# DMA transposes of the f16 parts of the probabilities in a two-layer hybrid attention encoder

## The chip, the cores and the metric

The kernel runs on one core of a Trainium2 chip, in one launch. The metric is the device time in microseconds; of the kernel before there are three runs, with a median of 2575.91 us (2571.5 to 2578.02).

## What is computed

An encoder of two layers runs for two requests: 512 tokens ("prompt") and 1024 tokens ("sample"), both of width 1024. All inputs are f32. Per layer:

```python
mod = jax.nn.silu(c) @ w_ada + b_ada
shift, scale, gate = jnp.split(mod, 3, axis=-1)
h = rms_norm(x, g_norm) * (1 + scale[:, None, :]) + shift[:, None, :]
proj = h @ w_in      # q_lat, kv_lat, k_rope, z_a, q_b, k_b, v_b, z_b
...
oa = block_attention(qa[:, :, None], ka, va, MLA_SCALE)      # 8 heads, keys of 96, values of 64
ya = heads_to_tokens(oa) * jax.nn.silu(z_a)
...
ob = block_attention(qb, kb, vb, GQA_SCALE)      # 8 heads of 64 over 2 key heads
yb = heads_to_tokens(ob) * jax.nn.silu(z_b)
out = jnp.concatenate([ya, yb], axis=-1) @ w_out
return x + gate[:, None, :] * out
```

`block_attention` is a full softmax over all keys, `softmax(q k^T * scale) v`, without a mask. A final RMSNorm follows the second layer.

## The kernel before

**Passes and tiles.** The work is four passes, `inst`: 0 is layer 0 of the prompt (512 keys), 1 is layer 0 of the sample (1024 keys), 2 and 3 are layer 1 of the same. A pass first makes keys and values for all its tokens (`key_steps`) and then goes through its query tiles of 128 tokens: 4 in a short pass, 8 in a long one (`over_tiles`, first tile, a loop of inner ones, last tile). Each engine has a program of its own, written by hand, in which the same loops run; semaphores tie them together. Nothing schedules the instructions but their order in those programs and the tables ahead of them.

**A head in a tile.** A tile has 16 slots, one per head: heads 0 to 7 are the latent attention (scores in f32, "A"), 8 to 15 the grouped-query attention (scores in f16 parts, "B"). In slot h of a long pass PE turns the probabilities of head h (`turn`, transposes of 128x128 f32 blocks through `ident` into two PSUM banks from `T_BANK`, four to a bank), forms the scores of head h+2 (`scores`), and multiplies the turned probabilities with V (`mix`, L770: three matmuls for each 128 keys, of high x high, high x low and low x high f16 parts). VectorE takes the row maximum of the scores (L1002), ACT the exponential into `probs` (L1163). ACT then copies the turned block as f16 into the high half of `PT` (`move_pt`, L1171) and VectorE writes the difference as f16 into the low half (`move_pt`, L1019). In a short pass `mix` runs one slot behind.

**Side products.** Between these stand the tile's other products, by tables of slots: z_a and z_b (gates of this tile), `out0`, `out1` (output projection of the tile before, in halves), and `PREPARE`, the queries of the next tile: h^T0 and h^T1 (transposes of the normed rows `xn`), q_lat, q_b, q_lat^T, q_up0 and q_up1, q_a^T and q_b^T. An entry stands before or after "|", that is ahead of or behind `mix` in its slot. All of them use the one PSUM bank `SIDE`; `side` makes PE wait on `mm_free` until VectorE has emptied it (`query_out`: L882 for h^T, L968 for the gates after ACT's tanh L1147, L973 for q_up). In VectorE's program the early entries of a slot stand ahead of the row maximum and the late ones behind it.

**Queues.** SP issues every DMA: a tile's rows into `xn` (L499, behind h^T1), its residual rows into `x_out` (L504), the result rows out (L507), and in the last tile of a pass the next pass's key weights (`key_weights`, with `query_weights` at the change of the layer). POOL norms and rotates the queries and forms the gates.

The line numbers in the rows: L577 is `product` (scores and side products), L567 the transpose helper (`turn`, h^T, q_a^T, y^T), L571 transposes of f16, L770 `mix`, L1028 the gated outputs, L1035 the final rows.

## Time and profile before

| | us |
|---|---|
| median of three runs | 2575.91 |
| span of the profiled execution | 2575.7 |
| PE busy | 2396.8 |
| VectorE busy | 1343.9 |
| ACT busy | 974.0 |
| POOL busy | 789.5 |
| one inner tile, 1024 keys (pass 1 / pass 3) | 92.40 / 93.45 |
| one inner tile, 512 keys (pass 2) | 72.24 |

The profiled execution's span is all that the page gives of its time; it lies 0.2 us under the median of the runs, and outside it nothing is counted. A tile here runs from one slot's product to the same one in the next tile, read from the chain. The page gives the busy time of each engine and the chain of work that ended last; windows of one tile, the chain's single pieces and a timeline around one place show what stands behind the shares.

### The profile page before, as it was taken

Reading aid. Unit: us, or ns where it says so; the run is one execution under the profiler, and the core shown is the slowest. Engines: PE = TensorE matmul, PEld = TensorE weight load, DVE = VectorE, ACT = ScalarE, POOL = GpSimd, SP = SyncE. Lnnn points to the kernel's source line nnn. Section 1 sums busy time; section 2 is a strip of 40 time slices with the busy share of each in tenths; the row PEclk is TensorE's granted clock in tenths of the full one; section 3 lists DMA queues with packets and bytes.
Section 4 is the critical chain, followed back from the end, with each engine's and each line's share of the span. In section 5 each row is a group of like instructions: output and inputs, shape, how many; then the busy total and the mean of one; then the engine's idle time right before and its main releaser. Section 6 shows DMA issues by size and latency. Waiting matters only on the chain.

```text
span 2575.7 us, 44323 instructions
## 1 busy us (share of the span) xinstructions
PE 2396.8 (93%) x16106; PEld 1409.9 (55%) x16106; DVE 1343.9 (52%) x2390; ACT 974.0 (38%) x2202; POOL 789.5 (31%) x1325
## 2 busy tenths in 40 slices
PE   6689999899999999999989899979899999999997
PEld 1344554455566566666555455545556656656654
DVE  0444444375656565555545444537555556555563
ACT  0223333133444444444422333422344444444442
POOL 0454321274421231232116632237442123123210
PEclk9799999899999999999999999999999999999999
DMA  7621112121000000000242000023000000000001
GB/s 237 222 96 58 54 52 85 58 94 38 9 9 25 16 24 8 24 17 0 73 155 98 9 17 25 33 101 122 9 9 10 33 24 16 24 33 25 0 25 41
DMA packets 63228, 129.42 MB, mean 50 GB/s; under 512 B 6687, under 2 KB 31365, under 8 KB 63125
## 3 DMA queue, kind: packets, MB, share of 16 engines
q1 hardware_dynamic: 63128, 128.09, 14.3%
q8 instruction: 64, 1.05, 0.2%
q14 instruction: 36, 0.29, 0.0%
HBM read 115.44 MB, written 12.63 MB: 50 GB/s over the span
## 4 chain that ended last, share of the span: by engine, by line
PE 75%; DVE 15%; issue 5%; ACT 2%; POOL 1%; DMA 1%; DVEq 0%; SPq 0%; POOLq 0%; ACTq 0%
PE psum L577 58%; PE psum L567 10%; PE psum L770 6%; DVE region L1019 3%; DVE nmax L1002 3%; DVE hT L882 3%; ACT region L1171 1%; DVE region L977 1%; DVE region L1028 0%; DVE region L979 0%; POOL region L1225 0%; PE psum L571 0%; ACT region L1147 0%; DVE KTa L944 0%; DMA Wq<-in_w_ada 0%
## 5 line engine op out<-in xcount | busy, mean ns | idle before, releaser
L1171 ACT ACTIVATE region<-psum 128x512 f16<-128x512 f32 x640 | 353.5, 594 | 769.2 <-PE psum L567 769.2
L577 PE MATMUL psum<-Wq,hT 128*128 128x512 f32 (+1 forms) x1536 | 611.0, 544 | 1.6 <-DVE hT L882 0.6
L1019 DVE TENSOR_TENSOR region<-psum,region 128x512 f16<-128x512 f32 x640 | 415.6, 682 | 293.4 <-ACT region L1171 292.8
L567 PE MATMUL psum<-ident,region 128*128 128x128 f32 (+1 forms) x3208 | 436.9, 277 | 21.5 <-DVE Va L917 10.5
L1002 DVE TENSOR_REDUCE nmax<-psum 128x1 f32<-128x1024 f32 (+1 forms) x384 | 398.6, 1038 | 41.9 <-PE psum L577 41.1
L577 PEld LDWEIGHTS psum<-Wq,hT 128*128 128x128 f32 x1536 | 285.0, 191 | 245.5 <-issue 224.9
L567 PEld LDWEIGHTS psum<-ident,region 128*128 128x128 f32 (+1 forms) x3208 | 356.5, 140 | 105.7 <-issue 78.6
L577 PE MATMUL psum<-Wout,region 128*128 128x512 f32 x768 | 354.5, 607 | 8.5 <-DVE region L987 6.7
L577 PE MATMUL psum<-KTa,region 96*128 96x512 f32 x640 | 311.9, 603 | 18.6 <-DVE region L977 12.9
L1225 POOL TENSOR_TENSOR region<-region,rope_sb 128x64 f32<-128x64 f32 (+3 forms) x384 | 158.3, 434 | 337.7 <-DVE region L973 321.3
L1163 ACT ACTIVATE region<-psum,nmax,unscale 128x1024 f32<-128x1024 f32 (+1 forms) x192 | 204.4, 1064 | 141.7 <-DVE nmax L1005 141.3
L1225 POOL TENSOR_TENSOR rsum<-sums,v_scale 128x8 f32<-128x8 f32 x48 | 9.7, 203 | 775.0 <-ACT region L1163 775.0
L577 PEld LDWEIGHTS psum<-Wout,region 128*128 128x128 f32 x768 | 143.9, 194 | 163.4 <-issue 145.4
L1163 ACT ACTIVATE region<-psum,nmax 128x1024 f32<-128x1024 f32 (+1 forms) x192 | 186.9, 973 | 114.1 <-DVE nmax L1002 112.2
L770 PEld LDWEIGHTS psum<-Vb,region 128*128 128x128 f16 x3840 | 136.6, 98 | 120.1 <-DVE region L1019 50.1
L770 PEld LDWEIGHTS psum<-Va,region 128*128 128x128 f16 x3840 | 136.7, 98 | 112.7 <-DVE region L1019 53.9
L770 PE MATMUL psum<-Vb,region 128*128 128x64 f16 x3840 | 152.6, 194 | 26.2 <-DVE region L1019 13.4
L577 PE MATMUL psum<-KTb,region 128*128 128x512 f16 x640 | 169.5, 379 | 1.2 <-DVE region L961 1.2
L577 PE MATMUL psum<-region,hT 128*128 128x416 f32 x384 | 149.5, 545 | 20.5 <-DVE hT L882 20.3
L968 DVE SCALAR_TENSOR_TENSOR region<-region,psum 128x512 f32<-128x512 f32 x48 | 33.0, 688 | 251.7 <-ACT region L1147 251.7
L577 PEld LDWEIGHTS psum<-KTa,region 96*128 96x128 f32 x640 | 108.7, 192 | 93.5 <-issue 81.0
L770 PE MATMUL psum<-Va,region 128*128 128x64 f16 x3840 | 148.3, 193 | 10.6 <-DVE region L1019 5.9
(110 smaller groups left out, 2156.3 us busy)
## 6 DMA issues: line engine op xcount, KB each, us to landing
Wout<-in_w_out SPq DMA_DIRECT2D x8, 2048.0 KB, 11.9
Va<-in_w_ada SPq DMA_DIRECT2D x12, 1024.0 KB, 5.4
Wq<-in_w_in SPq DMA_DIRECT2D x6, 2048.0 KB, 14.3
xn<-x_after_layer SPq DMA_DIRECT2D x24, 512.0 KB, 3.3
Wq<-in_w_ada SPq DMA_DIRECT2D x5, 2048.0 KB, 13.4
xn<-in_x_sample SPq DMA_DIRECT2D x16, 512.0 KB, 3.3
x_after_layer<-region SPq DMA_DIRECT2D x12, 512.0 KB, 2.6
region<-x_after_layer SPq DMA_DIRECT2D x12, 512.0 KB, 3.3
```

Of the source, the lines that this page charges most:

```text
L567: return nc.tensor.transpose(out, in_, ident[0:n, 0:n])
L577: last = nc.tensor.matmul(out, lhsTs[k], rhss[k], start=k == 0, stop=k == n - 1)
L770: last = nc.tensor.matmul(out, PT[:, a, pt_block(h, S, c), :], v, start=c == 0 and a + b == 0, stop=c == NT - 1 and a == 1)
L882: last = nc.vector.tensor_scalar(hT[:, k, :], ps[:, j * P:(j + 1) * P], gs[:, m, k:k + 1], cols[:, 16 * m + k:16 * m + k + 1], ALU.mult, A ...
L968: last = nc.vector.scalar_tensor_tensor(out=half, in0=half, scalar=1.0, in1=ps, op0=ALU.add, op1=ALU.mult)
L977: last = nc.vector.tensor_copy(QTa[0:QK, 4 * c:4 * c + 4, :], blocks[0:QK])
L1002: last = nc.vector.reduce_max(nmax[:, h:h + 1], scores_buf(h, S), AX_X, negate=True)
L1019: nc.vector.tensor_tensor(PT[:, 1, pt_block(h, S, 4 * c):pt_block(h, S, 4 * c) + 4, :], psum[:, T_BANK + b, :].rearrange("p (c n) -> p c n ...
L1163: nc.scalar.activation(probs_buf(h, S), scores_buf(h, S), ACT.Exp, bias=nmax[:, h:h + 1], scale=scale, accum_out=sums[:, h:h + 1]).then_in ...
L1171: nc.scalar.activation(PT[:, 0, pt_block(h, S, 4 * c):pt_block(h, S, 4 * c) + 4, :], psum[:, T_BANK + b, :].rearrange("p (c n) -> p c n", ...
L1225: mul = lambda out, a, b: nc.gpsimd.tensor_tensor(out, a, b, ALU.mult)
```

## The change

**The path of the probabilities.** PE no longer turns them. ACT copies the f32 exponentials from `probs` as f16 into the first half of a buffer `P16` (`high_part`), VectorE writes the f16 difference into the second half (`low_part`), and SP issues one DMA transpose of [128, 2S] f16 from `P16` into `PT` (L550), one a head: 256 of 512 KB and 128 of 256 KB in all. Room is for 2S = 2048 columns: two heads of 1024 keys, four of 512 (`buffers`). SP waits for the low part and for `pv_done` of the head that used the buffer before; each buffer has a semaphore `pt_loaded`, for which `mix` waits once, and ACT's copy of a later head waits on it too before it overwrites `P16`.

**The lead.** In slot h PE forms the scores of head h+4 (`AHEAD_SCORES`), VectorE takes the maximum of h+4 and the low part of h+2 (`AHEAD_TURN`), ACT the exponential and copy of h+3 (`AHEAD_PROBS`). `mix` runs in its own slot in all passes.

**The side products.** `PREPARE` moves one slot earlier (q_b^T stays), `LEFT_OVER` and `ADA` too; on POOL the norm of the latent and the rotations stand one slot earlier. VectorE has the outputs and the early entries ahead of the low part, then the maximum, then the late entries.

**The queues.** The loads of layer 1's modulation weights in pass 0 and the next pass's key weights (at the change of the layer the query weights with them) are issued by ACT: the latter in slot 5 of the last tile of passes 0 and 1, behind waits for the scores and for z_b. SP's loop over tiles is written out. The second half of `Wout` is loaded one key step earlier.

```diff
@@ -58,13 +58,16 @@
 FINISH = {2: "y_b^T |", 10: "| out0/0", 11: "out0/1 |", 12: "| out1/0", 13: "out1/1 |"}
 GATE_A = {0: "| z_a/0", 1: "z_a/1 |"}
 GATE_B = {2: "| z_b/0", 3: "z_b/1 |"}
-PREPARE = {4: "h^T0 |", 5: "h^T1 |", 6: "q_lat |", 7: "| q_b/0", 8: "q_b/1 |", 9: "q_lat^T | q_up0",
-           10: "q_up1 |", 12: "q_a^T0 |", 14: "q_a^T1 |", 15: "q_b^T0 | q_b^T1"}
+PREPARE = {3: "| h^T0", 4: "h^T1 |", 5: "q_lat |", 6: "| q_b/0", 7: "q_b/1 |", 8: "q_lat^T | q_up0",
+           9: "q_up1 |", 11: "q_a^T0 |", 13: "q_a^T1 |", 15: "q_b^T0 | q_b^T1"}
 TURN = {14: "| y_a^T"}
 
-LEFT_OVER = {5: "| q_b^T0@0 q_b^T1@0"}
-
-ADA = {0: "ada0 |", 7: "ada1 |", 11: "| ada2"}
+LEFT_OVER = {3: "| q_b^T0@0 q_b^T1@0"}
+
+AHEAD_SCORES, AHEAD_PROBS, AHEAD_TURN = 4, 3, 2
+P_ROOM = 2 * SMAX
...
@@ -138,8 +141,9 @@
...
-    trounds = [t // 4 for t in tiles]
-    tr_before = [sum(16 * tiles[p] * trounds[p] for p in range(q)) for q in range(len(inst))]
+    buffers = [P_ROOM // SEQS[r] for _, r in inst]
+    loads_before = [[sum(2 * HEADS * tiles[p] // buffers[p] for p in range(q) if b < buffers[p])
+                     for b in range(max(buffers))] for q in range(len(inst))]
...
@@ -280,30 +286,51 @@
...
+        def parts_buf(q, h):
+
+            S = SEQS[inst[q][1]]
+            b = h % buffers[q]
+            return P16[:, 2 * b * S:2 * (b + 1) * S]
+
+        def pt_buf(q, h):
+
+            S = SEQS[inst[q][1]]
+            b = h % buffers[q]
+            return PT[:, 2 * b * S:2 * (b + 1) * S].rearrange("p (c n) -> p c n", n=P)
+
+        def pt_value(q, i, h):
+
+            n = buffers[q]
+            return 16 * (loads_before[q][h % n] + i * (2 * HEADS // n) + h // n + 1)
+
+        def wait_pt(eng, q, i, h):
+
+            value = pt_value(q, i, h)
+            if not isinstance(value, int) or value > 0:
+                eng.wait_ge(pt_loaded[h % buffers[q]], value)
...
@@ -360,13 +387,34 @@
...
+        def load_key_weights(eng, q):
+
+            l, r = inst[q]
+            w_in_l = w_in[l].rearrange("(k p) n -> p k n", p=P)
+            eng.dma_start(Wkv[:, :, 0:KV_KB], w_in_l[:, :, C_KV:C_ZA]).then_inc(s["wkv_loaded"], 16)
+            eng.dma_start(Wkv[:, :, KV_KB:KVC], w_in_l[:, :, C_KB:C_ZB]).then_inc(s["wkv_loaded"], 16)
+            if l and r == 0:
+                query_weights(eng, l)
...
@@ -518,21 +543,26 @@
...
+                def turn(h, i):
+
+                    sp.wait_ge(s["p_low"], heads(b0, i, h))
+                    wait(sp, "pv_done", heads(b0, i, h - buffers[q]))
+                    sp.dma_start_transpose(pt_buf(q, h), parts_buf(q, h)).then_inc(pt_loaded[h % buffers[q]], 16)
+
                 def tile(i, first, last):
                     for h, names in enumerate(completed(first, last, q == 0)):
+                        if h + AHEAD_TURN < 2 * HEADS or not last:
+                            turn(h + AHEAD_TURN, i)
                         if last and h == 4 and q + 1 < len(inst):
                             first_rows(q + 1)
-                            if l < DEPTH - 1:
-                                key_weights(q + 1)
                         for name in names:
                             side(name, owner(name, i))
 
 
-                tile(0, True, False)
-                with tile_loop(sp, 1, NT - 2, rounds=(rounds, PER_SIDE + (len(ADA) if q == 0 else 0))) as i:
-                    tile(i, False, False)
-                tile(NT - 2, False, False)
-                tile(NT - 1, False, True)
+                for h in range(AHEAD_TURN):
+                    turn(h, 0)
+                for i in range(NT):
+                    tile(i, i == 0, i == NT - 1)
...
@@ -730,7 +759,7 @@
...
-                    if h in (0, 1, 4, 8):
+                    if h in (0, 4, 8):
                         pe.wait_ge(s["mm_free"], rounds.now() - later)
                     j = h - HEADS
...
@@ -761,43 +778,37 @@
...
+                    wait_pt(pe, q, i, h)
                     for c in range(NT):
-                        if c % 4 == 0:
-                            pe.wait_ge(s["pt_low"], tr_before[q] + nr * heads(0, i, h - 1) + c // 4 + 1)
-
                         for a, b in ((0, 0), (0, 1), (1, 0)):
                             v = Va[:, c, b, head, :] if head < HEADS else Vb[:, c, b, g * GD:(g + 1) * GD]
-                            last = nc.tensor.matmul(out, PT[:, a, pt_block(h, S, c), :], v, start=c == 0 and a + b == 0,
+                            last = nc.tensor.matmul(out, pt_buf(q, h)[:, a * NT + c, :], v, start=c == 0 and a + b == 0,
                                                     stop=c == NT - 1 and a == 1)
                     last.then_inc(s["pv_done"], 1)
 
                 def tile(i, first, last):
                     for h, (before_mix, after_mix) in enumerate(slots(first, last, q == 0)):
-                        turn(h, i)
-
-                        side_first = delay or any("^T" in name or "_up" in name for name in before_mix)
+
+                        side_first = any("^T" in name or "_up" in name for name in before_mix)
                         if side_first:
                             for name in before_mix:
                                 side(name, i)
-                        later = 0 if first else 1
-                        if h + 2 < 2 * HEADS:
-                            scores(h + 2, i, later)
+                        n = h + AHEAD_SCORES
+                        if n < 2 * HEADS:
+                            scores(n, i, 0 if first and n == 4 else 1)
                         elif not last:
-                            scores(h + 2 - 2 * HEADS, i + 1, later)
+                            scores(n - 2 * HEADS, i + 1, 0)
                         if not side_first:
                             for name in before_mix:
                                 side(name, i)
...
@@ -1006,19 +1016,18 @@
...
 
                 def next_max(h, i, last):
-                    if h + 2 < 2 * HEADS:
-                        row_max(h + 2, i)
+                    n = h + AHEAD_SCORES
+                    if n < 2 * HEADS:
+                        row_max(n, i)
                     elif not last:
-                        row_max(h + 2 - 2 * HEADS, i + 1)
-
-                def move_pt(h, i):
-
-                    for c in range(nr):
-                        b = c if nr == 2 else h % 2
-                        dve.wait_ge(s["pt_high"], tr_before[q] + nr * heads(0, i, h - 1) + c + 1)
-                        nc.vector.tensor_tensor(PT[:, 1, pt_block(h, S, 4 * c):pt_block(h, S, 4 * c) + 4, :],
-                                                psum[:, T_BANK + b, :].rearrange("p (c n) -> p c n", c=4),
-                                                PT[:, 0, pt_block(h, S, 4 * c):pt_block(h, S, 4 * c) + 4, :], ALU.subtract).then_inc(s["pt_low"], 1)
+                        row_max(n - 2 * HEADS, i + 1)
+
+                def low_part(h, i):
+
+                    dve.wait_ge(s["p_high"], heads(b0, i, h))
+                    parts = parts_buf(q, h)
+                    nc.vector.tensor_tensor(parts[:, S:2 * S], probs_buf(q, h), parts[:, 0:S], ALU.subtract) \
+                        .then_inc(s["p_low"], 1)
...
@@ -1039,28 +1048,26 @@
...
-                        if not delay:
-                            move_pt(h, i)
-                            for name in names[:early]:
-                                side(name, owner(name, i))
-                            next_max(h, i, last)
+                        for name in names[:early]:
+                            side(name, owner(name, i))
+                        if h + AHEAD_TURN < 2 * HEADS or not last:
+                            low_part(h + AHEAD_TURN, i)
+                        next_max(h, i, last)
                         for name in names[early:]:
...
@@ -1156,33 +1170,38 @@
...
-                    wait(act, "tr_ready", tr_before[q] + nr * heads(0, i, h - 1 - delay))
+                    wait(act, "p_low", heads(b0, i, h - buffers[q]))
                     if h % HEADS == 0:
                         wait(act, "gate_ready", 2 * (b0 + i) - 1 + h // HEADS)
                     scale = 1.0 if h < HEADS else unscale[:, l:l + 1]
-                    nc.scalar.activation(probs_buf(h, S), scores_buf(h, S), ACT.Exp, bias=nmax[:, h:h + 1], scale=scale,
+                    nc.scalar.activation(probs_buf(q, h), scores_buf(h, S), ACT.Exp, bias=nmax[:, h:h + 1], scale=scale,
                                          accum_out=sums[:, h:h + 1]).then_inc(s["exp_done"], 1)
 
-                def move_pt(h, i):
-
-                    for c in range(nr):
-                        b = c if nr == 2 else h % 2
-                        act.wait_ge(s["tr_ready"], tr_before[q] + nr * heads(0, i, h - 1) + c + 1)
-                        nc.scalar.activation(PT[:, 0, pt_block(h, S, 4 * c):pt_block(h, S, 4 * c) + 4, :],
-                                             psum[:, T_BANK + b, :].rearrange("p (c n) -> p c n", c=4),
-                                             ACT.Copy).then_inc(s["pt_high"], 1)
+                def high_part(h, i):
+
+                    wait_pt(act, q, i, h - buffers[q])
+                    act.wait_ge(s["exp_done"], heads(b0, i, h))
+                    nc.scalar.activation(parts_buf(q, h)[:, 0:S], probs_buf(q, h), ACT.Copy).then_inc(s["p_high"], 1)
+
+                def probabilities(h, i):
+                    exponentials(h, i)
+                    high_part(h, i)
+
+                def next_probabilities(h, i, last):
+                    n = h + AHEAD_PROBS
+                    if n < 2 * HEADS:
+                        probabilities(n, i)
+                    elif not last:
+                        probabilities(n - 2 * HEADS, i + 1)
...
...
-                        if not delay:
-                            move_pt(h, i)
-                        if h + 1 < 2 * HEADS:
-                            exponentials(h + 1, i)
-                        elif not last:
-                            exponentials(0, i + 1)
-                        if delay:
-                            move_pt(h, i)
+                        next_probabilities(h, i, last)
+                        if last and h == 5 and q + 1 < len(inst) and l < DEPTH - 1:
+                            act.wait_ge(s["scores_ready"], 16 * before[q + 1] - 8)
+                            act.wait_ge(s["mm_ready"], at["z_b"])
+                            load_key_weights(act, q + 1)
...
```

PE's order around h^T0, pass 1, an inner tile. Before, from the scores of the slot that follows h^T0 (`KTa`) over the product with V (`Va`) and the turn (`ident,region`) to h^T1 (`ident,xn`):

```order
L577 MATMUL psum<-KTa,region 128x512 x2
L766 REGISTER_ALU
L770 MATMUL psum<-Va,region 128x64 x12
L766 REGISTER_ALU
L770 MATMUL psum<-Va,region 128x64 x12
L747 REGISTER_ALU
L297 ISA
L567 MATMUL psum<-ident,region 128x128 x4
L297 REGISTER_ALU
L567 MATMUL psum<-ident,region 128x128 x4
L723 REGISTER_ALU
L567 MATMUL psum<-ident,xn 128x128 x4
```

The change, from the second half of z_b (`Wq,hT`) to the scores of head 8 (`KTb`):

```order
L607 MATMUL psum<-Wq,hT 128x512 x4
L785 MATMUL psum<-Va,region 128x64 x24
L752 REGISTER_ALU
L696 REGISTER_ALU
L597 MATMUL psum<-ident,xn 128x128 x4
L752 REGISTER_ALU
L597 MATMUL psum<-ident,xn 128x128 x4
L304 REGISTER_ALU
L607 MATMUL psum<-KTb,region 128x512 x4
```

Both groups of transposes of h now stand next to each other, behind the product with V, and the turned blocks and the scores that stood between them are gone from there.

PE's order at q_up in the same tile (`Wuq`). Before:

```order
L723 REGISTER_ALU
L577 MATMUL psum<-Wuq,region 128x384 x2
L747 REGISTER_ALU
L297 ISA
L567 MATMUL psum<-ident,region 128x128 x4
L297 REGISTER_ALU
L567 MATMUL psum<-ident,region 128x128 x4
L723 REGISTER_ALU
L577 MATMUL psum<-Wuq,region 128x384 x2
L577 MATMUL psum<-KTb,region 128x512 x4
```

The change:

```order
L785 MATMUL psum<-Vb,region 128x64 x24
L752 REGISTER_ALU
L607 MATMUL psum<-Wuq,region 128x384 x2
L752 REGISTER_ALU
L607 MATMUL psum<-Wuq,region 128x384 x2
L304 REGISTER_ALU
L607 MATMUL psum<-KTb,region 128x512 x4
```

The two halves of q_up, between which a head was turned, are neighbours now.

VectorE's order from the evacuation of z_b (L968, in the change L978) to that of h^T, pass 1, inner tile. Before, to h^T0:

```order
L991 REGISTER_ALU
L967 REGISTER_ALU
L968 SCALAR_TENSOR_TENSOR region<-region,psum 128x512
L1001 REGISTER_ALU
L1002 TENSOR_REDUCE nmax<-psum 128x1
L1018 ISA
L1019 TENSOR_TENSOR region<-psum,region 128x512
L1018 REGISTER_ALU
L1019 TENSOR_TENSOR region<-psum,region 128x512
L991 REGISTER_ALU
L882 TENSOR_SCALAR hT<-psum,gs,cols 128x128 x4
```

The change, to h^T1:

```order
L977 REGISTER_ALU
L978 SCALAR_TENSOR_TENSOR region<-region,psum 128x512
L1029 TENSOR_TENSOR P<-probs,P 128x1024
L1011 REGISTER_ALU
L1012 TENSOR_REDUCE nmax<-psum 128x1
L1001 REGISTER_ALU
L893 TENSOR_SCALAR hT<-psum,gs,cols 128x128 x4
L1001 REGISTER_ALU
L893 TENSOR_SCALAR hT<-psum,gs,cols 128x128 x4
```

The subtraction, once two instructions of 512 columns behind the maximum, is one of 1024 columns ahead of it, and both evacuations of h^T come behind the maximum, one after the other.

SP's order in an inner tile of pass 1 (`P` is P16, a `DMA_TRANSPOSE` one head; `xn` the next tile's rows, `region<-in_x_sample` the residual rows). Before:

```order
L504 DMA region<-in_x_sample 128x1024
L498 ISA
L499 ISA
L499 DMA xn<-in_x_sample 128x1024
L506 REGISTER_ALU
L507 DMA x_after_layer_1<-region 128x1024
```

The change:

```order
L550 DMA_TRANSPOSE region<-P 128x16x128 x9
L532 DMA x_after_layer_1<-region 128x1024
L550 DMA_TRANSPOSE region<-P 128x16x128 x5
L529 DMA region<-in_x_sample 128x1024
L550 DMA_TRANSPOSE region<-P 128x16x128 x2
L524 DMA xn<-in_x_sample 128x1024
```

The tile's three copies, once alone on the queue, now stand between its sixteen transposes.

## Rows read from the trace of the kernel before

**Rows 1.** The page: span, busy time by engine, and the chain by engine.

```profile
span 2575.7 us, 44323 instructions
...
PE 2396.8 (93%) x16106; PEld 1409.9 (55%) x16106; DVE 1343.9 (52%) x2390; ACT 974.0 (38%) x2202; POOL 789.5 (31%) x1325
...
PE 75%; DVE 15%; issue 5%; ACT 2%; POOL 1%; DMA 1%; DVEq 0%; SPq 0%; POOLq 0%; ACTq 0%
```

**Rows 2.** Windows of one query tile in passes 1, 2 and 3; columns ahead.

```profile
core 0: us, PE busy (x) PEld busy (x) DVE busy (x) ACT busy (x) POOL busy (x), PEclk, DMA share, GB/s
...
1066.50:1158.90 92.40, 91.92 (x716) 57.06 (x715) 52.54 (x81) 41.78 (x88) 21.07 (x29) 1.00 0.05 17
1485.00:1557.24 72.24, 69.53 (x427) 39.55 (x427) 34.18 (x66) 27.43 (x74) 21.80 (x31) 1.00 0.05 16
2101.85:2195.30 93.45, 92.28 (x715) 57.04 (x715) 53.63 (x82) 42.72 (x90) 21.80 (x31) 1.00 0.06 22
```

**Rows 3.** Grouped lines of pass 3's tile: busy us, mean ns | idle before.

```profile
L1019 DVE TENSOR_TENSOR region<-psum,region 128x512 f16<-128x512 f32 x32 | 20.5, 682 | 19.2 <-ACT region L1171 19.2
L1002 DVE TENSOR_REDUCE nmax<-psum 128x1 f32<-128x1024 f32 x16 | 19.4, 1214 | 0.3 <-PE psum L577 0.3
...
L1171 ACT ACTIVATE region<-psum 128x512 f16<-128x512 f32 x33 | 18.0, 594 | 48.9 <-PE psum L567 48.9
...
L1035 DVE SCALAR_TENSOR_TENSOR region<-region,rinv 128x1024 f32<-128x1024 f32 x1 | 1.3, 1276 | 0.0
...
L1097 ACT ACTIVATE xn<-xn,rinv 128x1024 f32<-128x1024 f32 x1 | 1.2, 1155 | 0.0
...
L973 DVE TENSOR_SCALAR region<-psum 128x384 f32<-128x384 f32 x2 | 1.1, 552 | 0.3 <-PE psum L577 0.3
```

**Rows 4.** Chain in the same tile: start us, length us, what.

```profile
2115.09 0.87 PE psum L567 x8
...
2121.12 0.70 PE psum L770 x24
...
2123.25 1.72 PE psum L577 x4
```

**Rows 5.** Chain in a tile of pass 2, the same columns.

```profile
1519.32 0.44 PE psum L567 x4
```

**Rows 6.** Waits in pass 3's tile: total us, times, longest.

```profile
PEld psum L770 <- DVE region L1019: 4.2, 10, 1.4
```

**Rows 7.** Timeline from z_b to h^T0 in that tile: start us, length us.

```profile
2121.15 0.60 ACT L1147 ACTIVATE region<-psum 128x512 f32<-128x512 f32 x1 [3.41 <-PE psum L577]
...
2121.78 0.69 DVE L968 SCALAR_TENSOR_TENSOR region<-region,psum 128x512 f32<-128x512 f32 x1 [4.30 <-ACT region L1147]
...
2124.72 1.35 DVE L882 TENSOR_SCALAR hT<-psum,gs,cols 128x128 f32<-128x128 f32 x4
```

**Rows 8.** DMA queue (packets, MB, share) and issues (KB each, us to landing).

```profile
q1 hardware_dynamic: 63128, 128.09, 14.3%
...
xn<-in_x_sample SPq DMA_DIRECT2D x16, 512.0 KB, 3.3
x_after_layer<-region SPq DMA_DIRECT2D x12, 512.0 KB, 2.6
...
region<-modulation SPq DMA_DIRECT2D x4, 512.0 KB, 9.8
```

**Rows 9.** Timeline of SP beside the last tile of pass 1.

```profile
1278.48 3.30 SPq L441 DMA_DIRECT2D Wq<-in_w_in  x2
1281.82 2.92 SPq L439 DMA_DIRECT2D Wuq<-in_w_uq  x1
1284.78 7.86 SPq L441 DMA_DIRECT2D Wq<-in_w_in  x2
```

**Rows 10.** Windows of 4 us at the end of pass 1, columns as in rows 2.

```profile
1321.00:1325.00 4.00, 2.27 (x30) 2.06 (x31) 2.04 (x4) 0.42 (x1) 1.04 (x1) 0.81 0.74 260
1325.00:1329.00 4.00, 4.00 (x14) 2.65 (x13) 3.23 (x9) 0.00 (x0) 0.00 (x0) 0.77 0.36 111
```

142 lines of the change are left out of this document (62 added, 80 removed).

## The prediction

> **What bounds the kernel now.** I read the page's chain first: TensorE is 75% of it and VectorE 15%, while PE is busy for 93% of 2575.7 us, ACT for 38%, POOL for 31% [rows 1]. So time on PE's path counts, and another engine only where PE waits for it. The windows of one query tile in each of three passes say how a tile looks: 92.40 us (pass 1, 1024 keys, layer 0), 93.45 us (pass 3, the same in layer 1) and 72.24 us (pass 2, 512 keys), with a granted clock of 1.00 throughout and POOL busy for some 21 us [rows 2]. How much of a long tile PE waits lies between 1.2 us (93.45 less its busy 92.28 [rows 2]) and 4.2 us (its weight loads waiting for the subtraction L1019 [rows 6]). I take 3.6 us in pass 3 and 2.6 in pass 1, whose tile is 1.05 us shorter. The kernel is nearly a row of matmuls without gaps; the other engines run in the shade of it. That is what the change disturbs, so I price the removed matmuls and then walk one tile for each wait that their removal uncovers.
>
> **Removed from PE.** A head with 1024 keys costs eight transposes, 0.87 us in the chain [rows 4], one with 512 keys four, 0.44 us [rows 5]. A long tile loses 16 x 0.87 = 13.9 us, a pass of eight long tiles 111; a short tile 16 x 0.44 = 7.0, a pass of four 28. Together 2 x 111 + 2 x 28 = 278 us. If nothing took its place, the time would be 2298; that is the floor, not a forecast.
>
> **ACT and VectorE about even.** ACT drops two copies (L1171) of 594 ns a head and adds one f16 copy of 128x1024; the nearest row is the scaling L1097 with 1155 ns. VectorE drops two subtractions (L1019) of 682 ns and adds one of 128x1024 with both inputs in SBUF; the nearest row is L1035, 1276 ns [rows 3]. Neither is taken as gain or loss: 16 x (1.16 - 1.19) and 16 x (1.28 - 1.36) are about zero. What matters is where they stand.
>
> **Waits that the transposes used to cover.** All side products go through one PSUM bank, so each waits until VectorE has emptied it of the one before. A transpose group and a score stood between two of them. Layer 0, long tile, one by one:
> - z_b to h^T0: tanh on ACT 0.60, then the evacuation 0.69, from z_b's end at 2121.12 [rows 4] to 2122.47, 1.35 us [rows 7]; with a hand-over of 0.2 it is 1.55. Now only the product of 0.70 [rows 4] lies between: wait 0.9. z_a to y_b^T likewise: 0.9.
> - h^T0 to h^T1: they now stand side by side. VectorE empties z_b, then does the subtraction (1.28 by L1035) and the maximum (1.21 by L1002) [rows 3], and only then the evacuation of h^T0 (four in 1.35 [rows 7]); pipelining takes 0.1 off each, a hand-over adds 0.2. Of some 3.7 us PE fills 0.4 with h^T0's own matmuls: wait 3.1 to 3.3, taken 3.1. Before, a score of 1.72, a product of 0.70 and a group of 0.87 lay there [rows 4].
> - q_lat^T to q_up0 and q_up0 to q_up1, also side by side, each behind a subtraction or maximum of 1.2 and an evacuation of 0.55 (L973 [rows 3]): 1.7 each.
> - the scores of head 14, which wait for head 12's exponential: 1.2. q_a^T0, q_a^T1 and q_b^T0, each behind an evacuation of 0.69 with nothing between: 0.9 each. Small ones: 0.3.
> Sum 12.5 us against 2.6 now: +9.9. In layer 1 I take 14.5 against 3.6, +10.9, since ACT's tanh can stand behind an f16 copy that waits for a landing (ACT is in order, and exponentials, tanh and squares queue behind that wait). A short tile gets 12.6 against 4: +8.6.
>
> **Filling and emptying.** At a pass's start the first product comes only after maximum, exponential, copy, subtraction and a transfer, 1.2 + 1.3 + 1.2 + 1.3 + 3.4 us, against four scores (4 x 1.72) that PE has to do; with the second head's share I take +10 for a long first tile and +8 for a last one, whose last heads have no scores ahead; +4 and +5 for short ones.
> - pass 1: -111 + 10 + 6 x 9.9 + 8 = -34; pass 3: -111 + 10 + 6 x 10.9 + 8 = -28.
> - passes 0 and 2: -28 + 4 + 2 x 8.6 + 5 = -2 each, pass 0 with +4 for the three extra side products of its tiles.
> Sum -62 us.
>
> **The transfers.** No transpose by DMA is in this trace. Copies of 512 KB land in 2.6 us (stores), 3.3 (loads) and 9.8 (the gate row spread over partitions, issued among weights) [rows 8]. I take 3.4, nearest to the loads, which like these are issued alone in a tile. In throughput they fit: 160 MiB more; the queue moved 128.09 MB in 14.3% of the span [rows 8], that is 348 GB/s, so one of 512 KB takes 1.5 us of data, 24 us of a tile of 88. What must fit is the landing: with two buffers, head n's transfer is issued after the product of head n-2, and its own product stands two slots later, 4.8 to 5.9 us at the tightest heads (6, 9, 10, 15 and 0). 3.4 fits there with hand-overs; beyond some 3.7 it does not. SP, in order, now has the tile's three copies between transposes; what they wait for (a bank emptied, a store landed after 2.6) is over before the next transpose is due.
>
> The Trainium skill, "DMA: Bandwidth & Descriptors", section "Latency and other measured facts", gives a DMA transpose 261 GB/s in one measured case, and by that 512 KB would be an estimated 0.5 us later; by the slope of the late rival below the sum would be 2586 instead of 2558. No run here shows it yet.
>
> **Issues moved to ACT.** Beside pass 1's last tile SP held its queue for 3.30 + 2.92 + 7.86 us to issue the next layer's query weights [rows 9]; ACT now does that at slot 5, in front of its exponentials. PE has four scores and some side products in hand: of 14 us I count 10 (bounds 0 and 15). The modulation loads on ACT in pass 0 are 11 short issues on an engine that is idle for half of a tile: nothing.
>
> **The clock.** Where PE was idle for a good part of some us, the granted clock fell afterwards: 2.27 us busy of 4 at 0.81, then 4.00 at 0.77, means of 2.4 and 1.2 GHz [rows 10]; that cost 4 x 0.19 + 4 x 0.23 = 1.7 us. The 3 to 4 us without matmuls around h^T are such a place, and 20 tiles have one: +34 (bounds 0, as in tiles now, and 68 with a second fall in each).
>
> **Sum.** -62 + 10 + 34 = -18 us on a span of 2575.7; the median of the runs is 2575.91, so nothing is added: **2558**.
>
> **Rivals.**
> 1. Transfers land late: slower. If a transpose needs data at half the copy rate, or SP holds its queue for each, it lands in 4.9 us (SP was held 2.92 us by one load of 768 KB [rows 9], so a second and a half is near). Walking the tile with that, products 0 and 6 and the scores of heads 4 and 14 wait for 3.3 us more in an inner long tile, 7 in a first, 7.6 in a last; 2.7 in all of a short pass: 2 x (6 x 3.3 + 7 + 7.6) + 2 x 2.7 = +74, and some six more clock falls +10: 2642. It decides from 3.7 to 3.8 us on, at 56 us for each us. For it: a transpose writes 128 rows from each of its 16 column blocks and need not run as a copy does; against: the rows of the copies. At 6 us and more every head waits and the time passes 2700.
> 2. The clock stays up and the weights' issue hides: 2576 - 62 = 2514. For it: a granted clock of 1.00 in the tiles now; against: rows 10.
> 3. The subtraction and POOL hinder each other. Both its inputs are now in SBUF; POOL works 21.8 of 93.45 us [rows 2], so of 16 x 1.28 = 20.5 us of subtractions 4.8 coincide; if those take double, a fifth lies on PE's path, 1 us in each of 24 tiles: 2582. The Trainium skill, "SBUF — State Buffer", section "Who interferes with whom", lets VectorE's second port and GpSimd exclude each other. No row of this trace shows it.
>
> **How the numbers follow.** Own case (2530 to 2590) 0.40; rival 2 0.15; rival 1 0.28, and past 2700 another 0.08; rival 3 0.09. A measurement here can tell about 0.3%, 7.7 us. Faster than 2568: 0.29 of my own case and rival 2, 0.44. Within: 0.09 of my own and 0.05 of rival 3, 0.14. Slower: rival 1 with its tail 0.36, 0.04 of rival 3 and 0.02 of mine, 0.42. Range 2505 to 2680: below it some 0.06 of rival 2, above it the tail and 0.05 of rival 1.
>
> **What would show it.** L567 with region inputs gone but for q_a^T and y^T; inner long tiles of 88 to 90 us; idle time of PE before the two h^T groups (some 4 us a tile) and before q_up0 and q_up1, put down to VectorE's evacuations; ACT silent for 14 us in pass 1's last tile; clock rows under 1.00 just behind h^T; landings of 3 to 4 us in the DMA table. Landings over 4 us, with PE's products waiting for them, would show it wrong on the slow side; a clock of 1.00 in every tile on the fast side.

## The result, and the profile after

The change makes the kernel slower: median **2689.76 us** (2684.45 to 2696.83) against 2576.11 in the same comparison, a ratio of 1.0447 (95% interval 1.0427 to 1.0467). The forecast was 2558 with a range up to 2680; the sign was wrong and the time lies above the range.

The page of the profile after, with the issues of the transposes, answers to [rows 1] and [rows 8]:

```profile
span 2685.6 us, 38154 instructions
...
PE 2235.6 (83%) x13546; PEld 1189.5 (44%) x13546; DVE 1358.0 (51%) x2134; ACT 985.4 (37%) x1946; POOL 885.1 (33%) x1325
...
q1 hardware_dynamic: 710744, 272.84, 46.0%
q10 hardware_dynamic: 20032, 23.07, 2.5%
...
PE 57%; DVE 15%; issue 10%; POOL 9%; DMA 5%; ACT 2%; ACTq 1%; SPq 0%; DVEq 0%; POOLq 0%
...
region<-P SPq DMA_TRANSPOSE x384, 4.3
```

The 2560 transposes are gone (16106 to 13546 matmuls), which were worth 278 us. PE's busy time fell by 161 only, so the matmuls that are left took 117 us longer; and PE's idle time, span less busy, rose from 179 to 450 us, by 271. -161 + 271 = +110, the whole difference of the spans (the medians differ by 114). The chain went the same way: PE from 75 to 57%, with issue, POOL and DMA in its place.

The longer matmuls are the clock. The mean granted clock, after and before:

```profile
core 0: 2685.6 us, clock 0.924
```

```profile
core 0: 2575.7 us, clock 0.980
```

It stands at either 2.4 or 1.2 GHz, so the time at the lower level is 2 x (1 - 0.924) x 2685.6 = 408 us after and 103 before.

By place, in us, each tile from product to product in the trace. Filling runs from the pass before, over the key stage, to the first product with V; in pass 0 it starts with the span. The forecast column is the prediction's own terms, the clock and ACT's hold included:

| place | before | after | change | forecast |
|---|---|---|---|---|
| pass 0, filling + first tile | 169.5 + 67.7 | 166.9 + 65.6 | -4.7 | -0.3 |
| pass 0, two inner tiles, mean | 83.6 | 87.0 | +3.4 | +4.3 |
| pass 1, filling + first tile | 145.8 + 77.4 | 153.8 + 82.0 | +12.6 | -2.2 |
| pass 1, six inner tiles, mean | 92.4 | 92.0 | -0.4 | -2.3 |
| pass 1, last tile | 79.6 | 101.4 | +21.8 | +4.1 |
| pass 3, filling + first tile | 144.5 + 77.4 | 154.6 + 80.4 | +13.1 | -2.2 |
| pass 3, six inner tiles, mean | 93.3 | 95.0 | +1.7 | -1.3 |
| pass 3, last tile | 79.9 | 79.7 | -0.2 | -5.9 |
| pass 2, filling + first tile | 99.1 + 63.1 | 102.6 + 69.6 | +10.0 | -1.3 |
| pass 2, two inner tiles, mean | 72.1 | 79.3 | +7.2 | +3.3 |
| pass 2, last tile | 56.0 | 70.4 | +14.4 | -2 |
| pass 0, last tile | 61.3 | 75.8 | +14.5 | -1 |

The forecast is a change of the span by -18 us, measured are +110: the 128 us between them are some 55 in last tiles, 37 in filling and first tiles and 36 in inner ones. Windows of the last tile of pass 0 before, then after of the last tile of pass 0, an inner and the last tile of pass 1 and the last of pass 2 (columns as in [rows 2]):

```profile
404.30:465.60 61.30, 57.96 (x387) 30.63 (x384) 26.46 (x48) 22.55 (x48) 6.29 (x8) 1.00 0.27 89
```

```profile
406.40:482.20 75.80, 61.19 (x347) 27.54 (x343) 26.06 (x48) 22.24 (x44) 6.48 (x8) 0.88 0.54 126
901.60:994.10 92.50, 82.72 (x590) 44.53 (x586) 51.54 (x66) 41.47 (x72) 25.42 (x29) 0.94 0.55 108
1270.00:1371.40 101.40, 64.16 (x516) 34.98 (x513) 39.03 (x45) 33.59 (x47) 6.48 (x8) 0.77 0.77 194
1702.10:1772.50 70.40, 52.17 (x299) 25.75 (x295) 25.90 (x46) 23.98 (x49) 11.02 (x14) 0.82 0.44 91
```

The inner tile of pass 1 now idles 9.8 us where it idled 0.5 [rows 2], and in the last tile of pass 1 PE stands for 37 us of 101.

The place that the prediction walked first, from z_b to h^T1 and the score behind it, in the timeline after (start us, length us; in brackets the idle time before it and its releaser):

```profile
1019.71 0.60 ACT L1161 ACTIVATE region<-psum 128x512 f32<-128x512 f32 x1 [2.55 <-PE psum L607]
...
1020.34 0.69 DVE L978 SCALAR_TENSOR_TENSOR region<-region,psum 128x512 f32<-128x512 f32 x1 [7.41 <-ACT region L1161]
1020.94 1.22 DVE L1029 TENSOR_TENSOR P<-probs,P 128x1024 f16<-128x1024 f32 x1
...
1021.15 0.65 PE L597 MATMUL psum<-ident,xn 128*128 128x128 f32 x4 [0.78 <-DVE region L978]
...
1022.08 1.22 DVE L1012 TENSOR_REDUCE nmax<-psum 128x1 f32<-128x1024 f32 x1
...
1023.21 1.36 DVE L893 TENSOR_SCALAR hT<-psum,gs,cols 128x128 f32<-128x128 f32 x4
...
1024.62 1.12 PE L597 MATMUL psum<-ident,xn 128*128 128x128 f32 x4 [2.82 <-DVE hT L893]
```

h^T0 waits 0.78 us (0.9 in the forecast). Then VectorE does the subtraction L1029 and the maximum L1012 ahead of the evacuation L893, and h^T1 waits 2.82 us (3.1). Its four matmuls take 1.12 us where h^T0's took 0.65: the clock has fallen in that wait. The inner tile of the window above has two such stretches, behind the wait for h^T1 and behind one of 1.81 us for VectorE's output L1037:

```profile
931.90:935.00 3.10, 3.00 (x19) 1.84 (x20) 1.89 (x6) 1.07 (x2) 0.00 (x0) 0.54 0.51 93
...
954.00:965.00 11.00, 10.35 (x90) 5.62 (x91) 7.55 (x10) 6.96 (x24) 3.42 (x5) 0.69 0.50 92
```

### The profile page after: what moved, and what is told of

Read it like the earlier page. It is cut to its first block, busy times and chain, and to the rows that moved or that the text cites. A ratio compares the mean times of both kernels' runs of the same rounds, so it can differ in the third digit from the quotient of the medians.

```text
span 2685.6 us, 38154 instructions
## 1 busy us (share of the span) xinstructions
PE 2235.6 (83%) x13546; PEld 1189.5 (44%) x13546; DVE 1358.0 (51%) x2134; ACT 985.4 (37%) x1946; POOL 885.1 (33%) x1325
## 4 chain that ended last, share of the span: by engine, by line
PE 57%; DVE 15%; issue 10%; POOL 9%; DMA 5%; ACT 2%; ACTq 1%; SPq 0%; DVEq 0%; POOLq 0%
PE psum L607 49%; POOL region L1246 4%; PE psum L785 4%; DMA region<-P 4%; PE psum L597 3%; DVE P L1029 3%; DVE hT L893 3%; DVE nmax L1012 2%; ACT region L1161 1%; POOL rsum L1406 1%; DVE region L1037 1%; DVE region L978 1%; POOL Wout L1246 1%; POOL rinv L1265 1%; DVE region L997 1%
## 5 line engine op out<-in xcount | busy, mean ns | idle before, releaser
L1184 ACT ACTIVATE P<-probs 128x1024 f16<-128x1024 f32 (+1 forms) x384 | 351.1, 914 | 374.1 <-DMA region<-P 356.1
L1029 DVE TENSOR_TENSOR P<-probs,P 128x1024 f16<-128x1024 f32 (+1 forms) x384 | 433.5, 1130 | 60.1 <-ACT P L1184 59.9
L1012 DVE TENSOR_REDUCE nmax<-psum 128x1 f32<-128x1024 f32 (+1 forms) x384 | 398.9, 1039 | 23.8 <-PE psum L607 22.1
L1264 POOL TENSOR_TENSOR rinv<-stat,eps 128x1 f32<-128x1 f32 (+2 forms) x120 | 23.1, 193 | 1142.6 <-ACT junk L1095 1129.0
L607 PE MATMUL psum<-KTa,region 96*128 96x512 f32 x640 | 329.9, 632 | 36.0 <-ACT probs L1177 28.2
L1177 ACT ACTIVATE probs<-psum,nmax,unscale 128x1024 f32<-128x1024 f32 (+1 forms) x192 | 202.5, 1055 | 409.8 <-DVE nmax L1015 390.1
L1177 ACT ACTIVATE probs<-psum,nmax 128x1024 f32<-128x1024 f32 (+1 forms) x192 | 185.0, 963 | 296.2 <-DVE nmax L1012 288.7
L1246 POOL TENSOR_TENSOR region<-region,rope_sb 128x64 f32<-128x64 f32 (+3 forms) x384 | 202.1, 547 | 208.2 <-DVE region L983 191.8
L607 PE MATMUL psum<-KTb,region 128*128 128x512 f16 x640 | 204.9, 442 | 36.4 <-ACT probs L1177 35.9
L978 DVE SCALAR_TENSOR_TENSOR region<-region,psum 128x512 f32<-128x512 f32 x48 | 33.0, 688 | 378.1 <-ACT region L1161 378.1
L785 PEld LDWEIGHTS psum<-Va,region 128*128 128x128 f16 x3840 | 153.8, 104 | 141.2 <-issue 98.9
L997 DVE TENSOR_TENSOR region<-psum,region 128x512 f32<-128x512 f32 x48 | 33.2, 691 | 278.4 <-PE psum L607 269.6
L597 PE MATMUL psum<-ident,region 128*96 128x128 f32 (+1 forms) x648 | 105.4, 286 | 68.8 <-DVE region L997 25.1
```

Source lines behind the costliest of these rows:

```text
L597: return nc.tensor.transpose(out, in_, ident[0:n, 0:n])
L607: last = nc.tensor.matmul(out, lhsTs[k], rhss[k], start=k == 0, stop=k == n - 1)
L785: last = nc.tensor.matmul(out, pt_buf(q, h)[:, a * NT + c, :], v, start=c == 0 and a + b == 0, stop=c == NT - 1 and a == 1)
L978: last = nc.vector.scalar_tensor_tensor(out=half, in0=half, scalar=1.0, in1=ps, op0=ALU.add, op1=ALU.mult)
L997: last = nc.vector.tensor_tensor(half, ps, half, ALU.add)
L1012: last = nc.vector.reduce_max(nmax[:, h:h + 1], scores_buf(h, S), AX_X, negate=True)
```

## The experiments

Each was timed beside the kernel before; ratios are to the kernel before, and gains to the 2689.76 us of the changed kernel.

**Side products over three banks.** The waits are said to come from the one PSUM bank of the side products. `banks` spreads these over banks 7, 4 and 5, so that PE waits only for the evacuation of the one before last.

```diff
         T_BANK, O_BANK, SIDE = 4, 6, 7
+        SIDE_BANK = {"z_a": 7, "y_b^T": 4, "z_b": 7, "h^T0": 4, "h^T1": 7, "q_lat": 5, ...}
...
-                        pe.wait_ge(s["mm_free"], rounds.now() - between)
-                    last = query_product(name.split("@")[0], owner(name, i), psum[:, SIDE, :], half)
+                        full = name in ("q_lat", "q_up0") or name == "out0" and between or q == 0 and name == "q_a^T0"
+                        pe.wait_ge(s["mm_free"], rounds.now() - (between if full else 1))
+                    last = query_product(name.split("@")[0], owner(name, i), psum[:, SIDE_BANK[name.split("@")[0]], :], half)
```

> The changed kernel with the side products spread over PSUM banks 7, 4 and 5 (4 and 5 lie idle since the turned blocks are gone), so that a side product waits only for the evacuation of the one before the last; q_lat and the first q_up, which read what was evacuated last, still wait for it. Theory A (the miss of the forecast is the clock, which falls because PE waits for the one side bank): PE's idle time in an inner long tile falls from some 10 us to under 4, the clock stays up there, the tile takes 81 to 84 us instead of 92, a short one 66 to 71 instead of 78 to 87; in all 2500 to 2560 us. Theory B (the transfers, which land after 4.3 us, set the pace): the waits move from the bank to the transposes, a long tile keeps 88 us or more, the whole 2640 or more.

Measured: 2583.44, ratio 1.0028 (1.0019 to 1.0038): 106 us back, the largest part found. First tiles of the long passes went from 82.0 and 80.4 to 72.8 and 72.2, five of six inner tiles of pass 1 to between 85.4 and 87.4 (one 93.0). Neither theory has its time: 2583 lies between 2560 and 2640. An inner tile of pass 1 with `banks`:

```profile
960.20:1045.60 85.40, 77.52 (x592) 43.11 (x589) 50.88 (x66) 41.47 (x72) 26.06 (x29) 1.00 0.59 117
```

The clock is 1.00 there and the matmuls take 77.5 us, but over the whole execution it hardly rose:

```profile
core 0: 2585.8 us, clock 0.927
```

So the gain came from the waits and not from the clock. In the tile 7.9 us of idle time are left; PE's waits in it (us in total, times, longest):

```profile
PE psum L610 <- DVE hT L899: 2.9, 1, 2.9
PE psum L789 <- DVE region L1043: 2.7, 2, 2.2
PE psum L610 <- ACT probs L1183: 2.1, 2, 1.3
```

The first is the scores of head 8, which wait for the evacuation of h^T; the second the products of heads 8 and 0, which wait until VectorE has emptied the one bank of the outputs; the third scores that wait for an exponential. No product waits for a transpose there, but the chain of that tile (start us, length us, what) goes over two landings, where the changed kernel's goes over one:

```profile
1008.62 4.26 DMA region<-P
...
1040.19 4.27 DMA region<-P
```

So the single bank of the side products was the first cause; behind it stand other evacuations and, in the chain, the transfers.

**Keeping PE busy in the waits.** `fill` issues dummy transposes ahead of the waits, to see what the clock alone costs.

```diff
+        FILL = {'h^T0': 6, 'h^T1': 26, 'q_up0': 12, 'q_up1': 12, 'y_b^T': 6, 'q_a^T0': 6, 'q_a^T1': 6, 'q_b^T0': 6}
...
+                        for _ in range(FILL.get(name.split("@")[0], 0)):
+                            transpose(psum[:, 5, 0:P], ident[:, :])
```

> The changed kernel with dummy transposes of the identity into the idle bank 5 placed ahead of the waits for the side bank: 26 of them ahead of h^T1, 12 ahead of each q_up, 6 ahead of h^T0, y_b^T, q_a^T and the first q_b^T, each group shorter than the wait it stands in. They are read by nobody. Theory A (the clock): the stretches at 1.2 GHz in the tiles (309 of 408 us of half clock) fall to under 150 us in the whole run, an inner long tile takes 88.5 to 90 us, the whole 2610 to 2650 us, though PE has more to do. Theory B (transfers) and a theory C (the last tiles' queues): nothing or some us more, 2685 to 2720 us.

Measured: 2668.31, ratio 1.0364 (1.0346 to 1.0381), 21 us back. The mean clock rose from 0.924 to 0.953, 251 us at the lower level instead of 408. An inner tile of pass 1, one of four of the six with this length (the others took 91.6 and 95.0):

```profile
1085.60:1175.60 90.00, 87.01 (x674) 51.74 (x671) 51.36 (x66) 41.66 (x73) 25.99 (x29) 1.00 0.56 111
```

It takes 90.0 instead of 92.5 us at a clock of 1.00. In the changed kernel its matmuls took 82.7 instead of the 78.0 that are left of 91.9 [rows 2] without 13.9 of transposes, 4.7 us more; only 2.5 of them come back. Idle time and dummies together are 90.0 - 78.0 = 12.0 us now, where the slower matmuls had left 9.8: the rest had lain in the waits, or is dummies that outlasted theirs; the run does not part the two. Short inner tiles of pass 2 got longer, 81.4 instead of 79.3 us on the mean. The 2610 to 2650 of theory A did not come, nor its fall of the lower level to under 150 us.

**Where the query weights are issued.** `weights` takes the loads of layer 1's query weights from ACT in pass 1's last tile and gives them to SP, among the key steps of pass 2.

```diff
             eng.dma_start(Wkv[:, :, KV_KB:KVC], w_in_l[:, :, C_KB:C_ZB]).then_inc(s["wkv_loaded"], 16)
-            if l and r == 0:
-                query_weights(eng, l)
...
-                if q == 0:
+                if r == 0:
 
-                    query_weights(sp, 0, (0,))
+                    query_weights(sp, l, (0,))
```

> The changed kernel with the query weights of layer 1 (8.75 MB) no longer issued by ACT in the last tile of pass 1 but by SP among the key steps of pass 2, as layer 0 has it; the key weights (1.66 MB) stay on ACT. Theory C (ACT held by issues and transposes queued behind weights): that tile falls from 101.4 to 78 to 84 us, pass 2's key stage grows by at most 6; in all 2665 to 2678 us. Theory A alone: the tile was long from the clock, and it stays above 92 us.

Measured: 2662.58, ratio 1.033 (1.0308 to 1.0352), 27 us back. (By the rows of issues the five loads moved are 7936 KB, not 8.75 MB.) What stood there in the changed kernel, in the timeline of its last tile of pass 1:

```profile
1300.31 2.39 SPq L550 DMA_TRANSPOSE region<-P  x1
...
1306.37 6.22 ACTq L400 DMA_DIRECT2D Wq<-in_w_in  x2
...
1312.61 4.51 ACTq L398 DMA_DIRECT2D Wuq<-in_w_uq  x1
1317.15 8.10 ACTq L400 DMA_DIRECT2D Wq<-in_w_in  x2
1325.35 1.20 ACT L1177 ACTIVATE probs<-psum,nmax,unscale 128x1024 f32<-128x1024 f32 x1 [19.40 <-issue]
...
1326.70 1.89 PE L607 MATMUL psum<-KTb,region 128*128 128x512 f16 x4 [18.72 <-ACT probs L1177]
...
1341.27 1.46 PE L785 MATMUL psum<-Vb,region 128*128 128x64 f16 x24 [5.04 <-DMA region<-P]
```

ACT held 19.4 us by issues, PE waits 18.7 of them for its exponential. 15 us later a product waits another 5.0 us for a transpose among the arriving weights; its piece in the chain is 11.28 us long instead of 4.27. With `weights` the tile takes 81.3 us instead of 101.4, and the key stage of pass 2 102.9 instead of 102.6: the loads cost nothing where they stand now. The tile gives 20 of the 27 us; the rest is not located.

**Key weights later, or in pieces.** On top of `weights`, `late` lets SP issue the next pass's key weights behind the last transposes of a pass, and `pieces` has ACT issue them in eight pieces in slots 5 to 12.

```diff
-                    if l == DEPTH - 1:
-                        key_weights(q + 1)
+                    key_weights(q + 1)
...
-                        if last and h == 5 and q + 1 < len(inst) and l < DEPTH - 1:
-                            act.wait_ge(s["scores_ready"], 16 * before[q + 1] - 8)
-                            act.wait_ge(s["mm_ready"], at["z_b"])
-                            load_key_weights(act, q + 1)
```

> The kernel with the query weights among the key steps, and the key weights of passes 1 and 2 issued by SP behind the last transpose of the pass before, so that no weights of the next pass move in a last tile. Theory C' (weights and transposes in the same DMA engines): pass 0's last tile goes from 75.9 to 64 to 69 us, pass 1's from 81.3 to 77 to 79, and the key stages behind them grow by the load, 4 to 8 us each. If the tile is long because its heads follow each other without cover, it stays at 73 us or more, and only the key stages grow: slower than 2663 by 8 to 16.

```diff
+            for k in ks:
+                eng.dma_start(Wkv[:, k, 0:KV_KB], w_in_l[:, k, C_KV:C_ZA]).then_inc(s["wkv_loaded"], 16)
+                eng.dma_start(Wkv[:, k, KV_KB:KVC], w_in_l[:, k, C_KB:C_ZB]).then_inc(s["wkv_loaded"], 16)
...
-                        if last and h == 5 and q + 1 < len(inst) and l < DEPTH - 1:
+                        if last and 5 <= h < 5 + KD and q + 1 < len(inst) and l < DEPTH - 1:
```

> The kernel with the query weights among the key steps, and besides the 1.66 MB of key weights for passes 1 and 2 issued by ACT in eight pieces, one in each of slots 5 to 12 of the last tile instead of all in slot 5. Theory C' (in a last tile the transposes stand behind the weights in the same DMA engines): their landings of 9.6 and 6.0 us in pass 0's last tile go back to some 3 to 4, that tile from 75.9 to 64 to 70 us, pass 1's from 81.3 to 77 to 80; in all 2645 to 2655 against 2663. If the tile is long for want of cover alone, it stays within 2 us of 75.9.

Measured: `late` 2659.16, ratio 1.0323 (1.0306 to 1.034); `pieces` 2669.54, ratio 1.037 (1.0345 to 1.0395). Beside `weights` that is -3 and +7 us, and the intervals of the ratios overlap: no difference is shown. Pass 0's last tile went from 75.9 to 73.8 with `late` and to 77.1 with `pieces`, not to the 64 to 70 of theory C': traffic of weights is not what makes it 14 us longer. Pass 1's last tile went from 81.3 to 77.1 and 79.9, as that theory has it.

**The next pass's rows.** In a pass's last tile ACT squares and scales the first rows of the next pass; in the changed kernel it can stand there waiting for their load, with exponentials queued behind. `xsq` moves that three slots back, with POOL's root between the two.

```diff
-                        if last and q + 1 < len(inst) and h == 6:
+                        if last and q + 1 < len(inst) and h == 9:
                             x_square(2 * before[q + 1])
-                        if last and q + 1 < len(inst) and h == 8:
+                        if last and q + 1 < len(inst) and h == 11:
                             x_scale(2 * before[q + 1])
```

> The changed kernel with the next pass's first rows squared and scaled by ACT three slots later in a pass's last tile (slots 9 and 11 instead of 6 and 8, POOL's root in slot 10), since ACT runs three heads ahead and stood waiting there for the load of these rows. Theory C: the last tiles of passes 0 and 2 lose 4 to 8 us each, in all 8 to 16 us: 2674 to 2682. Theories A and B: no change of the whole beyond 3 us.

Measured: 2675.18, ratio 1.0397 (1.0375 to 1.0419), 15 us back. The last tile of pass 2 fell from 70.4 to 63.3 us; that of pass 0 did not move (75.6), so half of the 15 us is located. Window of pass 2's last tile with `xsq`:

```profile
1698.70:1762.00 63.30, 47.41 (x298) 22.96 (x294) 26.96 (x46) 23.92 (x49) 9.75 (x13) 0.92 0.49 101
```

**Smaller transfers.** `half` transposes only the high parts, 256 KB a long head instead of 512; the number of matmuls stays. It leaves the low part out of the result.

```diff
-                    sp.dma_start_transpose(pt_buf(q, h), parts_buf(q, h)).then_inc(pt_loaded[h % buffers[q]], 16)
+                    sp.dma_start_transpose(pt_buf(q, h)[:, 0:tiles[q], :], parts_buf(q, h)[:, 0:SEQS[r]]).then_inc(pt_loaded[h % buffers[q]], 16)
...
-                            last = nc.tensor.matmul(out, pt_buf(q, h)[:, a * NT + c, :], v, start=c == 0 and a + b == 0,
+                            last = nc.tensor.matmul(out, pt_buf(q, h)[:, c, :], v, start=c == 0 and a + b == 0,
```

> The changed kernel with DMA transposes of the high parts alone, 256 KB a head instead of 512 (128 instead of 256 with 512 keys); the product with V reads the high part in place of the low part, so the low part is left out of the result, while ACT and VectorE still do all their work. It should land in some 3.1 us instead of 4.3 and hold SP for 1.2 instead of 2.4. Theory B (the transfers cost by their landing): the chain's pieces of DMA and the waits of ACT's copy on landings shrink, a first and a last tile lose 3 to 6 us each, an inner long tile 1 to 3; in all 2635 to 2665 us. Theory A (only the side bank's waits and the clock): within 10 us of 2690.

Measured: 2649.34, ratio 1.029 (1.0264 to 1.0316), 40 us back for landings of 3.1 us instead of 4.3. The data and the issues are halved with them, and the run does not part these. Waits for the transposes (us in total, times, longest), changed kernel first, then `half`:

```profile
ACT P L1184 <- DMA region<-P: 356.1, 192, 8.9
...
PE psum L785 <- DMA region<-P: 41.2, 22, 5.0
```

```profile
ACT P L1184 <- DMA region<-P: 167.2, 200, 8.3
...
PE psum L785 <- DMA region<-P: 28.0, 17, 4.1
```

Most of these waits are ACT's, before its f16 copy, and mostly slack: they fell by 189 us, the time by 40. The queue's data went from 295.9 to 212.0 MB and its share from 48.5% of 2685.6 us to 31.8% of 2646.7, so 83.9 MB of transposes take 461 us of the 16 engines, **182 GB/s**.

**A copy for the subtraction.** `single` writes a plain f16 copy in place of the low part, so VectorE reads one SBUF input instead of two. It leaves the low part out of the result.

```diff
-                    nc.vector.tensor_tensor(parts[:, S:2 * S], probs_buf(q, h), parts[:, 0:S], ALU.subtract) \
+                    nc.vector.tensor_copy(parts[:, S:2 * S], probs_buf(q, h)) \
                         .then_inc(s["p_low"], 1)
```

> The changed kernel with VectorE's subtraction (two inputs in SBUF) replaced by a copy of the probabilities to f16 with one input; the low part is thereby left out of the result. Theory D (VectorE's second SBUF input slows POOL): POOL's 128x256 product by the rotation table goes from 916 ns back to some 731, the 128x1024 one on Wout from 2779 to 2354, POOL is busy for 790 to 800 us instead of 885, and the first tiles and pass 3's tiles, whose chain goes through POOL, lose 1 to 3 us each: 2660 to 2680 in all. If D does not hold, POOL's rows stay as they are.

Measured: 2666.43, ratio 1.0336 (1.0303 to 1.0369), 23 us back. Grouped lines of POOL's work and of the copy or subtraction, first of the kernel before, then after, then with `single`:

```profile
L1225 POOL TENSOR_TENSOR Wout<-Wout,region 128x1024 f32<-128x1024 f32 x32 | 74.4, 2354 | 0.0
L1225 POOL TENSOR_TENSOR region<-region,rope_sb 128x256 f32<-128x256 f32 x96 | 68.2, 731 | 7.0 <-POOL region L1225 5.7
```

```profile
L1029 DVE TENSOR_TENSOR P<-probs,P 128x1024 f16<-128x1024 f32 x256 | 325.9, 1274 | 59.5 <-ACT P L1184 59.4
...
L1184 ACT ACTIVATE P<-probs 128x1024 f16<-128x1024 f32 x256 | 270.5, 1057 | 362.0 <-DMA region<-P 355.8
...
L1246 POOL TENSOR_TENSOR Wout<-Wout,region 128x1024 f32<-128x1024 f32 x32 | 88.2, 2779 | 0.0
...
L1246 POOL TENSOR_TENSOR region<-region,rope_sb 128x256 f32<-128x256 f32 x96 | 86.0, 916 | 7.0 <-POOL region L1246 5.7
```

```profile
L1029 DVE CAST P<-probs 128x1024 f16<-128x1024 f32 x256 | 206.9, 809 | 76.2 <-ACT P L1184 76.1
...
L1246 POOL TENSOR_TENSOR Wout<-Wout,region 128x1024 f32<-128x1024 f32 x32 | 80.0, 2524 | 0.0
...
L1246 POOL TENSOR_TENSOR region<-region,rope_sb 128x256 f32<-128x256 f32 x96 | 70.6, 756 | 7.0 <-POOL region L1246 5.7
```

POOL's products, 731 ns before, take 916 on the mean in the changed kernel and 756 with the copy; POOL is busy for 828 us, not for 790 to 800. The mean of the subtraction hides that it suffers too. At the filling of pass 1, in the changed kernel and then with `single` (two subtractions or copies beside four of POOL's products, then one with no POOL work beside it):

```profile
625.85 11.24 POOL L1246 TENSOR_TENSOR Wout<-Wout,region 128x1024 f32<-128x1024 f32 x4
...
628.56 6.32 DVE L1029 TENSOR_TENSOR P<-probs,P 128x1024 f16<-128x1024 f32 x2
...
637.01 1.23 DVE L1029 TENSOR_TENSOR P<-probs,P 128x1024 f16<-128x1024 f32 x1 [1.00 <-ACT P L1184]
```

```profile
625.58 5.24 DVE L1029 CAST P<-probs 128x1024 f16<-128x1024 f32 x2
...
633.65 0.69 DVE L1029 CAST P<-probs 128x1024 f16<-128x1024 f32 x1 [1.70 <-ACT P L1184]
```

In the whole trace, 165 of the 256 long subtractions have no POOL work beside them and take 1217 ns on the mean; the longest beside it takes 3366. The copy, with its one input, is held in the same way. So `single` does not take the conflict away. It also shortens VectorE's step by 465 ns, and the 23 us are not divided between the two.

**Together, and further.** `combo` is `banks`, `weights` and `xsq` at once. `split` is `combo` with each transfer in two halves, the high part sent as soon as it is written. `combo2` is `combo` with the output in two banks, so that product 8 does not wait for VectorE to empty product 7's bank, the side products on two, and a score of head 8 that waits for less. `combo3` is `combo2` with `pieces`.

> The three changes together: side products over three banks, the query weights among the key steps, the next pass's rows later on ACT. If their causes are separate places of the time line, the gains add: 106 + 27 + 15 us off 2690, that is 2542 (2530 to 2555), faster than the kernel before by 1 to 2%.

Measured: 2554.1, ratio 0.9909 (0.9887 to 0.9931), 0.9% faster than the kernel before. 136 us back where the three alone add to 148: nearly independent.

```diff
-                    sp.wait_ge(s["p_low"], heads(b0, i, h))
...
+                    for a, name in ((0, "p_high"), (1, "p_low")):
+                        sp.wait_ge(s[name], heads(b0, i, h))
...
+                        sp.dma_start_transpose(pt_buf(q, h)[:, a * NT:(a + 1) * NT, :], parts_buf(q, h)[:, a * S:(a + 1) * S]) \
```

> The same three changes with each transfer cut in two, the high part issued as soon as ACT's copy is done, the low part after VectorE's subtraction, so that only 256 KB are left to land behind the subtraction. Theory B: with the side bank out of the way the landing is what an inner long tile waits for (three pieces of 4.3 us in its chain); each shrinks by some 1.2 us, a tile from 86.8 to 83 to 85, the whole to 2490 to 2525. If the landing is not what bounds, it stays at the time of the kernel with the three changes, or gets worse by the 384 further issues.

Measured: 2581.11, ratio 1.0018 (1.0005 to 1.0032), 27 us worse than `combo`, where 29 to 64 better were expected. Each half lands in 3.2 us, not in half of 4.3, and the mean clock fell from 0.939 to 0.919. That the second issue on SP gives the head start away is argued, not shown.

```diff
+        O_BANKS = (6, 5)
...
-                        wait(pe, "y_ready", 2 * (b0 + i) + h // HEADS)
-                    out = psum[:, O_BANK, (h % HEADS) * VD:(h % HEADS + 1) * VD]
+                        wait(pe, "y_ready", 2 * (b0 + i) + h // HEADS - 1)
+                    out = psum[:, O_BANKS[h // HEADS], (h % HEADS) * VD:(h % HEADS + 1) * VD]
...
-                            scores(n, i, 0 if first and n == 4 else 1)
+                            scores(n, i, 0 if first and n == 4 else 2 if n == 8 else 1)
```

> The kernel with the three changes, and the two groups of heads accumulate in PSUM banks of their own (6 and 5, the side products alternate between 7 and 4), so that the products of heads 8 and 0 need not wait until VectorE has read the outputs of the eight heads before; and the scores of head 8 wait for the evacuations that they need only, not for that of h^T0. Theory E (PE's waits ahead of these two products and of head 8's scores, 2.2 + 2.2 + 2.9 us in an inner long tile, have taken the place of the side bank's): an inner long tile of pass 1 falls from 86.8 to 80 to 84 us, one of pass 3 from 92 to 85 to 89, in all 2470 to 2520. Theory B (landings): the waits move on to the transposes and the tiles keep 85 us or more, 2530 or more.

Measured: **2495.51** (2487.18 to 2498.13), ratio 0.9682 (0.9659 to 0.9704): 3.2% faster than the kernel before, and by the medians 7.2% faster than the changed one. Inner tiles of passes 1, 2 and 3:

```profile
946.60:1030.70 84.10, 77.92 (x593) 43.21 (x589) 50.90 (x65) 41.58 (x72) 25.03 (x29) 1.00 0.61 118
1448.00:1514.80 66.80, 61.96 (x367) 33.32 (x364) 33.64 (x66) 28.15 (x71) 25.26 (x31) 1.00 0.41 79
2126.50:2212.00 85.50, 77.76 (x590) 43.23 (x587) 52.18 (x66) 42.39 (x74) 26.93 (x31) 1.00 0.61 123
```

The clock is at 1.00 in all three. 4.8 to 7.7 us of each are still idle. Over the whole execution it is 0.951.

> The same with the key weights in eight pieces. By theory C' 8 to 12 us less than without the pieces.

Measured: 2495.63, ratio 0.9708 (0.9675 to 0.9742): nothing beyond `combo2`, where 8 to 12 us were expected.

## Why the prediction was wrong, step by step

**The step that failed** is the price of what the removal uncovers. The prediction set 216 us of waits, 10 of ACT's hold and 34 of the clock, 260 in all, against the 278 removed. Measured are 271 us more of idle time and 117 of longer matmuls, 388 in all. The mechanism was named, the one bank of the side products above all. But it was walked for an inner tile only, and there set against a wait that did not exist; the ends of the passes, where 92 of the 128 us arose, got lump sums.

**Removed: right.** 278 us of transposes went; the busy time of an inner tile at full clock is 77.9 (`combo2`) against 91.9 [rows 2]. ACT's copy took 1057 ns (1155 taken) and VectorE's subtraction 1274 (1276 by [rows 3]).

**Waits in inner long tiles: right in the main places, the sum by luck.** 12.5 us were listed for layer 0. The tile of the window idles 9.8, with slower matmuls that shorten waits, and `fill` bounds it at 12.0. The six waits at y_b^T, h^T0, h^T1, q_a^T0, q_a^T1 and q_b^T0 were listed with 7.6 us and take 6.8. The two ahead of q_up were listed with 3.4 and take 0.65, that of head 14's scores with 1.2 and takes nothing. Not listed were the products of heads 8 and 0, which wait 1.8 and 0.4 us for VectorE's output L1037. The scores of head 8 waited only when the bank's wait was gone (2.9 us in `banks`); `combo2` took both kinds away.

What was wrong is the 2.6 us set against them as already there in pass 1, taken between 1.2 and 4.2: the window of the very tile shows 92.40 less 91.92, 0.5 us [rows 2]. The waits of the weight loads [rows 6] were not waits of PE. That is 2 us in each of the tiles of pass 1, and as much in pass 3, where 3.6 was taken against 1.2.

**The clock: undersized in extent.** 408 us at the lower level against 103, in 63 stretches of the trace against 18. The forecast took one fall per tile at h^T and none in last tiles or key stages; the tile of the window has two, the second behind the unlisted wait at product 8. Yet 117 us of longer matmuls are not 117 of time: where PE waits for something that ends by itself, slower matmuls before it only shorten the wait. `fill`, which removed 157 us of the 305 added, gave 21 back, though it may have put some dummies on the path; at that rate the 305 would be worth an estimated 41 us, near the 34 taken. What the clock alone costs is not shown more closely.

**Landing: 4.3 us, not 3.4.** The step took the nearest copies as the row, and the rate of copies, 348 GB/s [rows 8]. The transposes' 167.8 MB (295.9 - 128.1) fill 48.5% of 2685.6 us less 14.3% of 2575.7, 934 us, 180 GB/s; and SP was held for 2.39 us by the issue of one of them (1300.31 in the timeline of pass 1's last tile; 1.9 us is the median of the inner tiles of pass 1). That is rival 1 with both of its conditions, half the copy rate and a held queue; it was to decide from 3.8 us on, and 4.3 is beyond. Its slope was too steep: 40 us for 1.2 by `half`, 33 per us, not 56; so by an estimate rival 1 explains some 30 of the 128 us, and part of that is also in the rows below. The Trainium skill, "DMA: Bandwidth & Descriptors", section "Latency and other measured facts", has 261 GB/s for one case; these traces have 180 to 182, and the measurement decides.

**ACT's hold: 10 taken, 20 measured** in that tile, 27 by the run's time. The cover was to be four scores and some side products; the timeline has none of it, since PE's next score waits for an exponential behind the issues (18.72 us). The step counted the engine that is held, and left out the transposes behind the weights: one took 11.28 us in the chain instead of 4.27.

**Last tiles: +8 and +5 taken.** Pass 3's came 5.7 us above the forecast, the short ones 16. One cause is shown: ACT, in order, waited for the next pass's rows (`xsq`, 7 us in pass 2's tile). Pass 0's is 14.5 us longer by two parts. PE's idle time rose from 3.3 to 14.6 us, of which 10.2 are products that wait for transposes:

```profile
PE psum L785 <- DMA region<-P: 10.2, 5, 3.0
```

And its matmuls took 61.2 us where 51.0 were left (57.96 less 7.0 of transposes), at a mean clock of 0.88. What would shorten it stays open: `single` gives 3.4 us back, `banks` 3.2, `half` 3.1, `fill` 2.3, `late` 2.1, `xsq` none. A single tile can differ by more between two runs in which its code is the same (the second tile of pass 1 took 91.4 us in the changed kernel and 97.2 with `weights`). That the heads simply follow each other with too little matmul work between is argued, not shown.

**First tiles: the filling was near, the rest left out.** +10 were taken in all. From the first score to the first product the long passes take 7.2 us before and 15.1 after, +8.0; some 1.7 of that is a subtraction held by POOL, which the sum did not have. The same single-bank waits as in inner tiles were not added: `banks` takes 8 to 9 us off each first tile.

**Rival 3: the mechanism was there, and both lose.** 38 of the 384 subtractions took over 0.1 us longer than those without POOL beside them, some 35 us together, up to 3366 ns for 1217. POOL got slower too, on the mean 731 to 916 and 2354 to 2779 ns; its busy time rose by 96 us and its share of the chain from 1 to 9%. The rival had only VectorE's side and 1 us a tile. The Trainium skill, "SBUF — State Buffer", section "Who interferes with whom", says that a VectorE instruction with two SBUF inputs contends with a GpSimd instruction that reads SBUF. The trace agrees, with 6.32 us for two subtractions that take 1.22 each alone. How much of the 114 us this is, no run shows.

**Rival 2 was excluded** by a mean clock of 0.924 and by ACT's 19.4 us.

## What to carry to other kernels

When a full PE loses matmuls, what they covered comes into view: here PE's idle time rose by 271 us for 278 of matmuls removed. Before taking them away, double what is single (here the bank of the side products and the bank of the outputs), since the same change with two output banks, two side banks and the loads rearranged is 3.2% faster than before instead of 4.5% slower. (What these would give the kernel before was not run.) A load issued from an engine on the path can cost its full length, as ACT's 19.4 us did. So can a wait of an in-order engine for the next stage's data, in pass 2's last tile though not in pass 0's. A forecast should walk the first and the last tile of a pass like an inner one, and not take a lump sum.

## What the runs showed of the hardware

- A DMA transpose of 512 KB, SBUF to SBUF in f16, landed in 4.3 us and one of 256 KB in 3.1: halving it saves only 1.2. In throughput it ran at 180 to 182 GB/s, half of the copies' 348, and its issue held SP for 1.9 us as the median, 2.39 in one case shown.
- Weight loads issued by ACT held it for 19.4 us, and a transpose behind them took 11.3 us instead of 4.3.
- A VectorE subtraction with both inputs in SBUF and POOL's products held each other up: 1.2 us alone and up to 3.4 beside POOL, and POOL's products 18 to 25% longer on the mean. A copy with one input was held too, 0.69 us alone and 5.24 for two.
